# The second round's products with the values move from the block at 16 to the block at 18 of each recurrence pass

## The reference

```python
h = rmsnorm(x, norm_gain[l]); proj = h @ w_in[l]
# recurrence, per step and head
S = S * w_t + (-(S @ kk_t)) b_t^T + v_t k_t^T;  y_t = S r_t
# attention, per block of 128 queries and 256 keys
s = q @ k^T / 8 - slope * dist, masked to 0 <= dist < 128
prob = softmax([s, sink])[..., :-1];  o = prob @ v
x = x + concat(group_norm(y) * silu(g), o * silu(g)) @ w_out[l]
return rmsnorm(x, final_gain)
```

## Time and profile before

| | us |
|---|---|
| median of 3 runs | 1866.54 (1865.47 to 1867.09) |
| the profiled execution | 1869.03 |
| its span, first to last instruction | 1866.2 |
| TensorE busy in it | 1836.8 (98%) |
| VectorE busy | 1245.1 (67%) |
| ScalarE busy | 788.6 (42%) |
| GpSimd busy | 467.9 (25%) |
| mean granted TensorE clock | 0.996 |

### The profile page before, as it was taken

How to read it: one execution, slowest core, us unless ns; L and a number is a source line. 1 busy time by engine, 2 the same in 40 slices (tenths; PEclk the granted TensorE clock), 3 DMA queues, 4 the chain that set the end, 5 groups by cost and what they waited for, 6 DMA issues and landing times.

```text
span 1866.2 us, 38160 instructions
## 1 busy us (share of the span) xinstructions
PE 1836.8 (98%) x15008; PEld 1496.9 (80%) x15008; DVE 1245.1 (67%) x2255; ACT 788.6 (42%) x1578; POOL 467.9 (25%) x1096
## 2 busy tenths in 40 slices
PE   8999999999999999999999999999999999999996
PEld 5878888888888887888888888888888788878885
DVE  4676777777777678667777777677777754355333
ACT  6444444343534355444343534353534543242221
POOL 0005051423324150041423324150505060111110
PEclk9999999999999999999999999999999999999998
DMA  5533232333233325332333333333333543465443
GB/s 182 167 109 101 90 94 84 97 93 89 91 93 96 89 91 177 106 89 85 97 92 89 91 92 96 89 92 90 96 89 98 174 127 108 124 206 172 156 126 124
DMA packets 194963, 207.69 MB, mean 111 GB/s; under 512 B 98272, under 2 KB 101472, under 8 KB 194784
## 3 DMA queue, kind: packets, MB, share of 16 engines
q1 hardware_dynamic: 194784, 205.26, 36.8%
HBM read 183.18 MB, written 22.02 MB: 110 GB/s over the span
## 4 chain that ended last, share of the span: by engine, by line
PE 93%; DVE 4%; ACT 1%; DMA 1%; issue 1%; SPq 0%; DVEq 0%; ACTq 0%
PE psum L1184 76%; PE psum L1169 3%; PE psum L1313 2%; PE psum L1248 2%; PE psum L1286 1%; PE psum L1466 1%; PE psum L1347 1%; PE psum L1430 1%; PE psum L1273 1%; PE psum L1437 1%; PE psum L1210 1%; PE psum L1193 1%; DVE w_lo L754 1%; PE psum L1419 1%; DVE work L873 1%
## 5 line engine op out<-in xcount | busy, mean ns | idle before, releaser
L1184 PE MATMUL psum<-x_hi,w_hi 128*128 128x512 f32 x2144 | 871.7, 407 | 11.3 <-DVE x_lo L763 6.7
L1184 PE MATMUL psum<-x_hi,w_lo 128*128 128x512 f32 x2144 | 837.8, 391 | 0.0
L1184 PE MATMUL psum<-x_lo,w_hi 128*128 128x512 f32 x2144 | 837.1, 390 | 0.0
L754 DVE TENSOR_TENSOR w_lo<-w_raw,w_hi 128x512 fp32r<-128x512 f32 x536 | 371.6, 694 | 498.5 <-ACT w_hi L549 470.7
L549 ACT ACTIVATE w_hi<-w_raw 128x512 fp32r<-128x512 f32 x536 | 335.3, 629 | 774.9 <-PE psum L1184 692.3
L1184 PEld LDWEIGHTS psum<-x_hi,w_hi 128*128 128x128 f32 x2144 | 403.1, 188 | 111.3 <-issue 14.4
L1184 PEld LDWEIGHTS psum<-x_hi,w_lo 128*128 128x128 f32 x2144 | 402.6, 188 | 87.7
L1184 PEld LDWEIGHTS psum<-x_lo,w_hi 128*128 128x128 f32 x2144 | 403.6, 188 | 79.0 <-issue 4.1
L504 POOL TENSOR_TENSOR sub_t<-sub_l,sub_io 128x60 f32<-128x60 f32 (+24 forms) x496 | 187.4, 378 | 876.8 <-DMA sub_l<-scratch_L 839.2
L506 POOL TENSOR_TENSOR sub_io<-sub_io,sub_t 128x60 f32<-128x60 f32 (+24 forms) x496 | 201.6, 406 | 38.8
L526 POOL TENSOR_TENSOR v<-v,kb 128x512 f32<-128x512 f32 x29 | 38.3, 1321 | 266.4 <-ACT kb L698 266.1
(11 more groups left out here) (241 smaller groups left out, 1816.7 us busy)
## 6 DMA issues: line engine op xcount, KB each, us to landing
w_raw<-in_w_in SPq DMA_DIRECT2D x408, 256.0 KB, 2.6
w_raw<-in_w_out SPq DMA_DIRECT2D x128, 256.0 KB, 2.6
sub_l<-scratch_L SPq DMA_DIRECT2D x16, 512.0 KB, 4.4
stage<-in_x_t SPq DMA_DIRECT2D x20, 256.0 KB, 3.3
stage<-scratch_MIX SPq DMA_DIRECT2D x19, 256.0 KB, 3.5
late<-in_x_t SPq DMA_DIRECT2D x16, 256.0 KB, 3.1
scratch_MIX<-sa SPq DMA_DIRECT2D x16, 256.0 KB, 4.0
scratch_MIX<-ym SPq DMA_DIRECT2D x16, 256.0 KB, 3.2
```

Of the source, the lines that this page charges most:

```text
L754: nc.vector.tensor_tensor(w_lo[gq % SPLIT][:], w_raw[gq % RAW][:], w_hi[gq % SPLIT][:].bitcast(F32), ALU.subtract).then_inc(w_ready, 1)
L1184: mm = nc.tensor.matmul(psum[:, s % 2], wt[gq % SPLIT][:, cols], xx[:, c], start=(c == 0 and wt is w_hi and xx is x_hi), stop=(c == KC - 1 ...
```

## The change

The four lines that issue the second round's products with the values, with their waits, are moved within TensorE's `recurrence` from `at == 16`, where they stood in front of `under`, to `at == 18`, where they stand in front of `from_heads`. No other engine's program changes.

```diff
                     if at == 16:
-                        if i:
-                            pe.wait_ge(yt_read, i)
-                        pe.wait_ge(z_read, i + 1)
-                        values(i, 1)
                         pe.wait_ge(s_read, 2 * i + 2)
                         pe.wait_ge(x_back, 2 * 16 * (i + 1))
                         under(i)
...
                     if at == 18:
+                        if i:
+                            pe.wait_ge(yt_read, i)
+                        pe.wait_ge(z_read, i + 1)
+                        values(i, 1)
                         pe.wait_ge(lev_read, 2 * i + 2)
                         from_heads(4, xt, zs).then_inc(u_full, 1)
```

## The result

The changed kernel takes 1870.35 us (median of 11 executions, 1868.42 to 1872.94), the kernel before, run beside it, 1866.38 (11, 1865.11 to 1870.24): a ratio of 1.0018, 95% interval 1.001 to 1.0026. It is slower by about 0.2%, where the prediction had +1.0 us and a range up to 1869.7. The profiled execution took 1870.35, its span is 1868.3, 2.1 more than before. These two traces understate the change somewhat: the profiled execution of the kernel before took 1869.03, well above its median.

A forecast was written before the change was run, and what follows sets the result against it. TensorE was taken to bound the kernel, with VectorE setting the stalls of passes 6 and 14. Regular passes -1.26 and those two +2.26 summed to +1.0 us, median 1867.5, range 1864.1 to 1869.7.

The forecast's parts named there:

- What bounds it, and the places: TensorE is 93% of the span; only passes 6 and 14 stall at 17, 0.95 and 1.00 us, ended by VectorE.
- (a): Block at 16, which loses the values: 0.91 us instead of 2.13, so 1.22 less.
- (b): Block at 18, which gains the values in front of from_heads: 1.41 + 1.13 = 2.54 us.
- rival B: The wait carries the 0.09: values cost 1.22 at 18, regular passes gain 0, total 1868.9; chance 0.15.
- (c): Fourteen regular passes: -1.22 + 1.13 = -0.09 us each, together -1.26.
- (d): Passes 6 and 14: the 1.22 saved at 16 is lost in the stall at 17; block at 18 costs +2.26 together.
- The resumption stays: At 17 of passes 6 and 14, TensorE still resumes at 713.30 and 1447.87, set by VectorE.
- (e): Moved waits: DMAs for under and corner keep margins of 1.4 and 1.5 us; VectorE's level 0 and 1 no later.
- rival E: Clock falls in the stalls at 17 of passes 6 and 14: 2.9 us each, total +6.9, 1873.4; chance 0.05.
- Rival C: Stall at 17 not set by VectorE alone: all sixteen passes gain 0.09, -1.4, 1865.1; chance 0.10.
- D: Block at 16: under alone runs like corner, 0.21 us less per regular pass, total -1.9, 1864.6; chance 0.05.
- F: Returning DMA loads for under and corner late: each pass waits 0.3 us, +4.8, 1871.3; chance 0.03.

The follow-up runs named there:

- experiment 9: The changed kernel with the wait on lev_read ahead of the values instead of behind them; block at 18 measured 2.48 us, one execution.
- 10: The kernel before with the two waits of under moved ahead of the values; block at 16 measured 2.13 us, one execution.
- the regular half alone: Against the kernel before, values moved to 18 only in the fourteen regular passes, left at 16 in passes 6 and 14; 1865.08 us, ratio 0.9988.
- experiments 2: Against the kernel before, values moved to 18 only in passes 6 and 14; 1872.14 us, ratio 1.0023.
- experiments 5: The changed kernel with the values at 17 behind corner in passes 6 and 14, elsewhere at 18; 1865.66 us, ratio 0.9993.
- experiment 8: Values at 18 only in regular passes, plus VectorE emptying the r tile ahead of its kk work in passes 6 and 14; 1863.69 us, ratio 0.9981.

## Why the prediction was wrong

**What bounds it, and the places:** right. The regular passes have no stall, passes 6 and 14 have it, and VectorE sets its end.

**(a) the block at 16:** right, 0.91.

**(b) the block at 18:** nearly. 2.48 for 2.54. The values in front of `from_heads` cost 1.07, less than either end (1.13, 1.22): in the trace the first matmuls of `from_heads` start between the last ones of the values (365.20 beside 365.24), which in front of `under` (or of `turn_kk`) does not happen. That the 0.09 of the old place is not the wait was right (experiments 9 and 10), and rival B falls; that it is the change of tile shape agrees with all rows but was not tested by itself.

**(c)** fourteen passes: -0.15 each for -0.09, 2.1 us for 1.26. The run with the regular half alone shows 2.2 (0.6 to 3.9) against the kernel before.

**(d) passes 6 and 14:** the mechanism (the 1.22 is lost in the stall, the values stand behind it) was right, with 1.07 for 1.13 each. "The resumption stays" was not: with L787 at 0.91 instead of 0.69 VectorE ends 0.2 us later. So the stall of pass 14 here, and both stalls of experiments 2 and 9, are 2.39 to 2.45 where 2.2 was forecast, a term of +0.4 us for two passes that the sum lacks. In pass 6 of the changed kernel this does not show. There the stall grew by 0.67 and not by 1.2, since VectorE itself was faster (1.01 us for the four score multiplies that took 1.44, 0.48 for 0.67 on L918). In the run with the regular half alone these two took 1.44 and 0.67 again; what sets it was not tried. The chain in pass 6 also runs from GpSimd's inverse over the DMA queue and a weight load to `low` at 708.58, which waited 0.17 us for it: VectorE was then at the edge of not being the bound. All of this is worth under 1 us in one execution.

**(e) the moved waits:** right for the DMAs; no idle time ended by one anywhere at 16 or 17. VectorE's `level` 0, which was held to come no later, is the nearer bound: see pass 10 in experiments 5 and 9.

**The step that failed is rival E.** The prediction named it, with its place and its mechanism, and then gave it 0.05 and left it out of the sum and of the range. It happened in eight of ten profiled stalls of 1.6 us or more. The reason for the small chance was that the clock held through 0.95 us and that nothing showed a fall before the kernel's end; between the two stood 2.2 us, well over twice the longest idle time at that place. The nearest row of the kernel before, which the prediction did not use, is the 1.70 us at 1673.19, behind which the clock held; 2.2 lies beyond that too, and no row bounded it. A price of 6 us with an open condition should have had a chance near one half. Its size was off too, in the other direction, for the changed kernel: 2.9 us per stall was taken from the slow start of the kernel; 1.5 to 1.6 was measured there, though two of the eight falls on record cost 2.8. With the measured terms the sum is -2.1 + 2 x 1.07 + 2 x 1.55 = +3.1 (+3.6 with VectorE's 0.22 twice), against a measured 0.18% (0.10 to 0.26), which is 3.4 us (1.9 to 4.9).

What the Trainium skill says ("TensorE: Matmul & The Clock Gate", The HAM clock gate), that an idle stretch sends the array back to half rate, is what the trace shows: 0.50 in the stretches behind the stalls. The idle stretches that the section has in mind are longer than these; the measurement decides, and by it 1.62 to 2.45 us were enough in eight of ten. What the Trainium skill says of mode changes ("TensorEngine Tiling", Key Properties) agrees with the trace as far as it goes: one change less in each pass, and 0.09 us of the 0.15. That the drain is what the 0.09 pays for, no run here shows by itself.

Rival C (the stall isn't VectorE's) falls with experiment 8: moving VectorE's eviction alone takes the stall away. D falls with the block at 16, where `under` alone still takes 0.59 from its start to the next long matmul. F falls with (e).

## What to carry to other kernels

When work is taken out from in front of a stall that another engine ends, the stall grows by about as much and the work is paid in full where it now stands: look for stalls behind the place that is emptied, even if they are in two passes of sixteen. On TensorE add the price of the clock: if the lengthened stall goes beyond what the trace shows to be harmless, count the fall as likely: here eight of ten for an idle time of 1.62 to 2.45 us, at 1.5 to 1.6 us each and 2.8 in two of them. Such an exception is best handled by a condition on the pass or by shortening the stall at its source; both turned a loss of 0.18% into a gain of 0.12 to 0.19% (with the values inside the stall 0.07%, not clear of none).

## What was not expected of the hardware

The clock fell behind a stall of 1.62 us (pass 6 of the changed kernel) and held behind others of 2.39, 2.45, 1.70 and 1.61, so an idle time of this size decides nothing by itself. What else decides stays open. Executions of one kernel seem to differ by a fall or two, though only one of each has a trace: the eleven of the changed kernel have mean granted clocks of 0.996 (four, 1868.42 to 1869.68 us), 0.995 (four, 1868.72 to 1870.7) and 0.994 (three, 1870.54 to 1872.94). The fall also need not come at once: in pass 14 of the changed kernel five matmuls ran at full speed after the stall before it came, while in the run with the slowed VectorE the first one behind the stall was already slow (0.80 us), and in pass 6 of experiment 9 the granted clock was down before the stall ended at 711.71:

```profile
711.00:711.50 0.50, 0.00 (x0) 0.00 (x0) 0.50 (x1) 0.00 (x0) 0.00 (x0) 0.57 1.01 389
```
